# Requesting the cache pages of the compress stage during the input projection, and its first product as four 64x64 tiles

## The reference

```python
def compress(rows, pe, w1, w2):
    b, l, h, d = rows.shape
    nc = l // CMP_BLOCK                                   # CMP_BLOCK = 32
    blocks = rows.reshape(b, nc, CMP_BLOCK, h, d) + pe[None, None, :, None, :]
    flat = blocks.transpose(0, 1, 3, 2, 4).reshape(b, nc, h, CMP_BLOCK * d)
    return jax.nn.silu(flat @ w1) @ w2
```

## Time and profile before

| | before |
|---|---|
| time, median of 3 runs | 974.69 us (974.18 to 977.14) |
| the profiled execution's own time | 977.05 us |
| its span | 975.4 us |
| TensorE products (PE) | 918.1 us busy, 94% |
| TensorE weight loads (PEld, beside the products) | 692.2 us, 71% |
| VectorE (DVE) | 504.6 us, 52% |
| ScalarE (ACT) | 309.5 us, 32% |
| GpSimd (POOL) | 190.0 us, 19% |
| DMA | 91.11 MB, mean 93 GB/s |

### The profile page before, as it was taken

The page is one execution under the profiler, slowest core; times in us unless marked ns, Lnnn a source line. Parts: engine busy times, 40 slices in busy tenths (PEclk is TensorE's granted clock), DMA queues, the critical chain, the costliest instruction groups (busy, mean ns, idle before and its releaser), DMA issues. The chain is left out here.

```text
span 975.4 us, 15501 instructions
## 1 busy us (share of the span) xinstructions
PE 918.1 (94%) x5221; PEld 692.2 (71%) x5221; DVE 504.6 (52%) x1079; ACT 309.5 (32%) x691; POOL 190.0 (19%) x234
## 2 busy tenths in 40 slices
PE   7899999999999999999688898999999998989998
PEld 6676768887777787778588765566666655667784
DVE  4774254446165655340356366776666754564522
ACT  4222022213032424151200455655655543311100
POOL 1222222443002211110252001111011012443000
PEclk8999999999999999999899778999999999999999
DMA  7305811002530203113683500000000016888631
GB/s 264 133 19 106 226 29 59 1 2 86 211 103 1 87 10 122 44 50 106 149 193 99 151 1 23 22 23 23 1 23 10 13 31 208 234 227 293 212 97 48
DMA packets 90892, 91.11 MB, mean 93 GB/s; under 512 B 27629, under 2 KB 69533, under 8 KB 90453
## 3 DMA queue, kind: packets, MB, share of 16 engines
q1 hardware_dynamic: 70402, 71.60, 24.3%
q10 hardware_dynamic: 16700, 9.36, 3.6%
q0 software_dynamic: 3712, 9.17, 3.3%
HBM read 75.51 MB, written 23.49 MB: 101 GB/s over the span
## 5 line engine op out<-in xcount | busy, mean ns | idle before, releaser
L884 PE MATMUL ps<-w_high,x_high 128*128 128x512 f32 (+1 forms) x520 | 204.5, 393 | 2.3 <-DVE w_low L615 2.3
L886 PE MATMUL ps<-w_high,x_low 128*128 128x512 f32 (+1 forms) x520 | 199.5, 384 | 0.0
L885 PE MATMUL ps<-w_low,x_high 128*128 128x512 f32 (+1 forms) x520 | 199.1, 383 | 0.0
L884 PEld LDWEIGHTS ps<-w_high,x_high 128*128 128x128 f32 x520 | 97.8, 188 | 34.1 <-issue 12.9
L886 PEld LDWEIGHTS ps<-w_high,x_low 128*128 128x128 f32 x520 | 97.5, 187 | 21.0
L885 PEld LDWEIGHTS ps<-w_low,x_high 128*128 128x128 f32 x520 | 97.7, 188 | 18.9
L1721 PE MATMUL ps<-k_high,q_stack 128*128 128x512 f32 (+3 forms) x192 | 77.7, 408 | 11.9 <-DVE a_stats L1606 11.8
L399 POOL TENSOR_TENSOR stats<-stats,small 128x8 f32<-128x8 f32 (+3 forms) x35 | 41.7, 1190 | 206.4 <-DVE stats L667 158.5
L1721 PEld LDWEIGHTS ps<-k_high,q_stack 128*128 128x128 f32 x192 | 38.8, 202 | 53.3 <-DVE a_stats L1606 27.9
L1763 PE MATMUL ps<-weights_turned,v_nat 128*64 128x512 f32 x264 | 72.3, 629 | 0.0
L1722 PE MATMUL ps<-k_low,q_stack 128*128 128x512 f32 (+3 forms) x192 | 67.1, 356 | 0.0
(11 more groups left out here) (339 smaller groups left out, 1547.4 us busy)
## 6 DMA issues: line engine op xcount, KB each, us to landing
w_raw<-in_w_in SPq DMA_DIRECT2D x48, 256.0 KB, 4.5
tmp_skew<-tmp_table SPq DMA_DIRECT2D x8, 576.0 KB
bias_full<-tmp_skew SPq DMA_DIRECT2D x8, 512.0 KB, 4.8
w_out_raw<-in_w_out SPq DMA_DIRECT2D x16, 256.0 KB, 4.5
y_rows_in<-tmp_y SPq DMA_DIRECT2D x8, 512.0 KB, 4.8
x_rows<-in_x_prompt SPq DMA_DIRECT2D x8, 512.0 KB, 6.8
out_y_prompt<-out_rows SPq DMA_DIRECT2D x8, 512.0 KB, 6.7
x_tile<-in_x_prompt SPq DMA_DIRECT2D x6, 512.0 KB, 3.8
```

The source lines that it names most:

```text
L884: nc.tensor.matmul(out, s.xh[:, k, rows], s.wh[:, k, 0:w], start=(k == 0), stop=False)
L885: nc.tensor.matmul(out, s.xh[:, k, rows], s.wl[:, k, 0:w], start=False, stop=False)
L886: ins = nc.tensor.matmul(out, s.xl[:, k, rows], s.wh[:, k, 0:w], start=False, stop=(k == KT - 1))
```

## The change

1. The pages get room before the compress stage. Two units (`pages_early`) lie where `kct` and what follows it were; they are requested by SP in the q group. The other sixteen units, two of them prompt rows, lie in the columns of the input rows `x_high` and `x_low`: once zn has multiplied tile t, its columns are free, and two units go there. SP asks for four pages of each and POOL for the other four; ACT asks for none.
2. A page goes to 64 rows of SBUF, two consecutive rows of the page (two pieces of 512 bytes) to each, instead of 128 rows with one each. So two pages fill one 128-row tile, and its transposes give the even rows and the odd rows apart.
3. The prompt's rows are no longer transposed in the kv group; they are read back from the output `p_cmp_k` and `p_cmp_v` by SP in tiles 3 and 7 of zn, four requests each, as units like the others. So there are 18 units of two half units, 36 copies from PSUM, alternately on VectorE and ACT, over a ring of four banks.
4. The first product has no zeros: for each of 32 steps, four 64x64 products, two heads by even and odd block rows, into four quarters (two PSUM banks by upper and lower partitions). The weights stand in both halves of the partitions: SP loads them at the start of zn, VectorE copies them down in tiles 4 and 5. ACT copies one pair of quarters and VectorE adds the other to it, then silu follows.

The core of the diff:

```diff
+    s.w1 = Memory(nc, s.w_region).put("w1_doubled", [P, 2, CB, HD])
+    s.pages_early = Memory(nc, s.kct_region).put("pages_early", [P, EARLY, PAGES // 2, 2, KVW])
+    s.pages_in_x = [Memory(nc, s.x_region + 4 * KT * ROWS * part).put(f"pages_in_x{part}", [P, KT, ROWS]) for part in range(2)]
...
-                    if kind == "zn" and t < 2 * FIRST:
+                    if kind == "q" and t < 2 * EARLY:
                         if t == 0:
                             sp.wait_ge(table_in, 16)
-                            sp.wait_ge(w_low, KT * (g + 1))
-                        pool = io["cache_cmp_k"].rearrange("n t h d -> n t (h d)")
-                        for p in range(4 * (t % 2), 4 * (t % 2) + 4):
-                            at = PAGES * (t // 2) + p
-                            page = sp.value_load(s.pages[0:1, at:at + 1], min_val=0, max_val=N_PHYS - 1)
-                            sp.dma_start(s.raw_a[:, t // 2, p, :], pool[bass.ds(page, 1), :, :].rearrange("a t c -> (a t) c")).then_inc(s.c_first[t // 2], 16)
+                            sp.wait_ge(rows_in, 48)
+                            sp.wait_ge(r_out, TT)
+                        load_pages_paired(sp, s, io, t // 2, range(4 * (t % 2), 4 * (t % 2) + 4), s.early_in[t // 2])
+                    if kind == "zn" and t == 0:
+                        sp.wait_ge(w_low, KT * (g + 1))
+                        for kv, w1 in enumerate((io["cmp_w1_k"], io["cmp_w1_v"])):
+                            sp.dma_start(s.w1[0:HD, kv, :, :], dram(w1, 0, [HD, HD], [HD * HD, CB], [1, HD])).then_inc(s.w1_in, 16)
                     if kind == "zn":
                         sp.wait_ge(silu, NT + t + 1)
                         sp.dma_start(io["zn"][r0:r0 + n, :], s.st[0:n, slot, :]).then_inc(st_stored[slot], 16)
+                        if t < TT:
+                            for u in units_in(t):
+                                if is_prompt(u):
+                                    load_prompt_rows(sp, s, io, u, s.tile_in[t])
+                                else:
+                                    load_pages_paired(sp, s, io, u, SP_PAGES, s.tile_in[t])
...
+                    if kind == "zn" and t < TT:
+                        pool.wait_ge(table_in, 16)
+                        pool.wait_ge(projected, i + 1)
+                        for u in units_in(t):
+                            if not is_prompt(u):
+                                load_pages_paired(pool, s, io, u, POOL_PAGES, s.tile_in_sw[t])
...
+                    if KIND[g] == "zn" and t in (4, 5):
+                        dve.wait_ge(s.w1_in, 32)
+                        nc.vector.tensor_copy(s.w1[HD:P, t - 4, :, :], s.w1[0:HD, t - 4, :, :]).then_inc(s.w1_ready, 1)
...
                 if kind == "kv":
-                    for j in range(2):
-                        last = nc.tensor.transpose(s.ps[:, 3, P * j:P * j + n], st[:, KVW * j:KVW * j + KVW], one)
-                    last.then_inc(k_turned, 1)
...
-SLOTS, FIRST = 8, 4
-SP_PAGES, ACT_PAGES, POOL_PAGES = range(0, 3), range(3, 5), range(5, 8)
+EARLY, SEQS = 2, B + 1
+SP_PAGES, POOL_PAGES = range(0, 4), range(4, PAGES)
+is_prompt = lambda u: u % SEQS == B
+units_in = lambda t: (EARLY + 2 * t, EARLY + 2 * t + 1)
+
+
+def tile_of(s, u, q):
+
+    if u < EARLY:
+        return s.pages_early[:, u, q]
+    t, part = (u - EARLY) // 2, (u - EARLY) % 2
+    return s.pages_in_x[part][:, 2 * q:2 * q + 2, P * t:P * t + P]
+
+
+def load_pages_paired(engine, s, io, u, some, loaded):
+
+    pool = io[("cache_cmp_k", "cache_cmp_v")[u // SEQS]].rearrange("n t h d -> n t (h d)")
+    for p in some:
+        at = PAGES * (u % SEQS) + p
+        page = engine.value_load(s.pages[0:1, at:at + 1], min_val=0, max_val=N_PHYS - 1)
+        rows = slice(HD * (p % 2), HD * (p % 2) + HD)
+        engine.dma_start(tile_of(s, u, p // 2)[rows], pool[bass.ds(page, 1), :, :].rearrange("a (r two) c -> (a r) two c", two=2)).then_inc(loaded, 16)
+
+
+def load_prompt_rows(engine, s, io, u, loaded):
+
+    rows = io["prompt_out"][("cmp_k", "cmp_v")[u // SEQS]]
+    for q in range(PAGES // 2):
+        engine.dma_start(tile_of(s, u, q), dram(rows, 2 * KVW * P * q, [2 * KVW, P], [KVW, 2], [1, KVW])).then_inc(loaded, 16)
...
-        def load_pages(engine, u, some, loaded):
-
-            kv, b = u // B, u % B
-            if u >= SLOTS:
-                engine.wait_ge(turned, 2 * (u - SLOTS + 1))
-            for p in some:
-                page = engine.value_load(s.pages[0:1, PAGES * b + p:PAGES * b + p + 1], min_val=0, max_val=N_PHYS - 1)
-                engine.dma_start(raw(u)[:, p, :], pool_dram[kv][bass.ds(page, 1), :, :].rearrange("a t c -> (a t) c")).then_inc(loaded[u % SLOTS], 16)
...
-            b, half = i // 2 % B, i % 2
-            return view(kcs[:, 0, NBP * b + 16 * half:NBP * b + 16 * half + 1], [1, 16], [ALL, CB])
+            b = i // 2 % SEQS
+            return kcs[:, i % 2, :, NBP * b:NBP * b + NBP]
 
         def bank_of(i):
-            return view(s.ps[:, i % 3, 0:1], [CB, 16], [1, CB])
+            return view(s.ps[:, i % RING, 0:1], [1, CB // 2], [CB // 2, NBP])
...
+            def half_sums(kv):
+                act.wait_ge(first_out, 2 * kv + 2)
+                if kv == 1:
+                    act.wait_ge(silu_out, 1)
+                for h in range(HKV):
+                    frm = slice(HD * (1 - h), HD * (1 - h) + HD)
+                    nc.scalar.activation(both[HD * h:HD * h + HD, :], s.ps[frm, FIRST_BANK[kv][h], 0:ALL], ACT.Copy).then_inc(halved, 1)
...
+            def sums(kv):
+                dve.wait_ge(halved, 2 * (kv + 1))
+                for h in range(HKV):
+                    at = slice(HD * h, HD * h + HD)
+                    ins = nc.vector.tensor_tensor(both[at, :], s.ps[at, FIRST_BANK[kv][h], 0:ALL], both[at, :], ALU.add)
...
+            def turn(u):
+                landed(u)
+                for odd in range(2):
+                    i = 2 * u + odd
+                    if i >= RING and odd:
+                        pe.wait_ge(evacuated_a, kept_a(i - RING + 1))
+                    elif i >= RING:
+                        pe.wait_ge(evacuated, kept_v(i - RING + 1))
+                    for q in range(PAGES // 2):
+                        last = nc.tensor.transpose(s.ps[:, i % RING, P * q:P * q + P], tile_of(s, u, q)[:, odd, :], s.ident[:])
+                    last.then_inc(turned, 1)
...
-                for i in range(CB):
-                    if then and i % 4 == 0:
-                        turn_half(then + i // 4)
-                    last = nc.tensor.matmul(s.ps[:, 4 + kv, cols], w1[:, kv, i, :], kcs[:, i, cols], start=(i == 0), stop=(i == CB - 1))
+                    pe.wait_ge(position_kept, kv + 1)
+                pe.wait_ge(evacuated, kept_v(upto))
+                pe.wait_ge(evacuated_a, kept_a(upto))
+                for j in range(CB // 2):
+                    if then and j in (4, 10):
+                        for u in then.pop(0):
+                            turn(u)
+                    for odd in range(2):
+                        for h in range(HKV):
+                            at, to = slice(HD * h, HD * h + HD), slice(HD * odd, HD * odd + HD)
+                            last = nc.tensor.matmul(s.ps[to, FIRST_BANK[kv][h], cols], w1[at, kv, 2 * j + odd, :], kcs[at, odd, j, cols], start=(j == 0), stop=(j == CB // 2 - 1))
...
-            for i in range(B):
-                turn_half(i)
-            for kv in range(2):
-                for half in range(2):
-                    done = 2 * B * kv + B * (half + 1)
-                    first(kv, half, done if done < 4 * B else None)
-                    if kv == 1 and half == 0:
-                        second(0)
+            for u in range(4):
+                turn(u)
+            first(0, 0, [[4, 5], [6, 7, 8]])
+            first(0, 1, [[9, 10], [11, 12]])
+            first(1, 0, [[13, 14], [15, 16, 17]])
+            second(0)
+            first(1, 1, [])
```

More of the change, by code:

```diff
@@ L517, in post @@
                     br = 1 if kind == "wg" else 0
-                    act.wait_ge(k_turned, b + (1 if kind == "wg" else 2))
+                    act.wait_ge(k_turned, b + 1)
                     if t < TT:
@@ L1119, in compress @@
 def compress(nc, s, io):
-    m = Memory(nc, s.x_region)
[L1122 to L1126, removed]
+    ALL = NBS + NBP + 1
+    m = Memory(nc, s.w_region + 4 * 2 * CB * HD)
+    w1 = s.w1
+    kcs = m.put("kcs", [P, 2, CB // 2, ALL])
+    hid = m.put("hidden", [P, 2, NBS + NBP])
+    w2 = m.put("w2_blocks", [P, 2, P])
+    assert m.at <= SB_END
+    m = Memory(nc, s.rq_region + 4 * H * T + 4 * H * 2 * NBP)
+    both = m.put("both_parities", [P, ALL])
+    stat = m.put("c_stats", [P, 32])
+    assert m.at <= s.kct_region
+    m = Memory(nc, s.x_region)
     sq = m.put("c_squares", [P, 3, KVW])
@@ L1244, in _ @@
                 for j, (_, n) in enumerate(tiles):
+                    bank = OUT_BANK[j]
                     act.wait_ge(second_out, 3 * kv + j + 1)
```

(53 more changed lines are left out.)

127 lines of the change are left out of this document (45 added, 82 removed).

## The result

The changed kernel takes 999.62 us (996.38 to 1000.65, 4 runs), the kernel before 974.78 on the same chip: a ratio of 1.0248, interval 1.0221 to 1.0275. The profiled execution (996.38, span 994.7) is the shortest of the four, while that of before (977.05, span 975.4) was near the longest of its own; what the two traces differ by, 19.3 us, is therefore less than the 24.8 of the medians.

What follows compares the result with a forecast made beforehand. Projection was taken as bound by TensorE, compress by the arrival of pages, with SP all but full in zn. Barrier +46.1 us and compress -21.9 gave +24.2 on the median 974.69: 999 us, range 978 to 1020.

Steps and rivals of the forecast that it cites:

- SP's issue time: In zn, SP's page requests, stores and prompt reads last until 517.0, so barrier and compress come 46.1 us later.
- The price of the new request: In zn, a 64-row two-piece page request on SP was taken at 0.626 us, ends 0.338 and 0.697.
- a 64-row request costs no more: Rival, zn: a 64-row request costs SP no more than a 128-row one; +8.1 us, 983; chance 0.18.
- Compress: Compress stage: no idle time on pages, products four at once; 47.3 us against 69.2, 21.9 shorter.
- the wait for the last copy from PSUM: In compress, TensorE waits at four places for the last evacuation, 0.17 + 1.09, 4.7 us in all.
- The tail: End of compress: ACT copies and VectorE adds 0.45 each, hand-overs 0.4, silu 0.55, second product 1.0, copies 1.25 us.
- Transfers did not set the pace: Rival, zn: transfers, not requests, set the pace, until 487; shift 16.2, sum -5.7 us, 969; chance 0.05.
- Products run four at a time, not two: Rival, compress: only two products at once, 0.136 each; stage 64.5 us, sum +41.4, 1016; chance 0.10.
- TensorE was at half speed: Rival, compress: TensorE stays at half clock throughout; stage about 75 us, +52, 1027; chance 0.05.
- kv and q groups, silu, POOL: kv 1.8 us earlier, q nothing; in zn tile 7's silu about 488 and POOL's end 491, both before SP.

Runs made afterwards that it cites:

- 128 rows: Changed kernel, but a page goes to 128 rows of SBUF instead of 64 rows with two pieces: 986.99 us, ratio to before 1.0141.
- the three cures together: Changed kernel with 128-row pages, pages of zn tiles 0 to 5 shared by SP, ACT, POOL, tiles 6 and 7 behind the barrier: 952.52 us, ratio 0.9795.
- two quarters: Changed kernel, but both products of a head write that head's own quarter, using two quarters of TensorE, not four: 1017.23 us, one run.

## Why the prediction was right, point by point

**SP's issue time.** Forecast: through at 517.0; measured 517.1, and compress 46.5 later for 46.1. The runs above show the mechanism, not only the number: the same requests shared out, cheaper ones, or behind the barrier gave back 27, 10 and 22 us by the ratios, where 33, 10 and 25 to 30 were expected. The agreement to a tenth of a microsecond is luck: the eight tiles took 87.0 us for 85.3, and the first store went out at 429.6, where the sum began at 431.3, so two misses of 1.7 cancel. Inside the 87.0, too, terms missed both ways. The page was taken at 1.382 and cost 1.30 to 1.36 (10.08 - 0.54 over 7, or 9.62), because the request took 0.538 and not 0.626. Against that, the first tile took 13.7 us for 11.5 (its store alone 2.96, behind the two weight loads; why was not tested), a prompt read 0.61 for 0.51, and a store 0.59, for which 0.47 stood.

**The price of the new request.** 0.538 lies between the ends 0.338 and 0.697, nearer to the dear one; the rival "a 64-row request costs no more" falls. When the cheap request was put in (128 rows), SP was through 34.6 us later than before (505.5 for 470.88), not the 30.0 of that rival: the first tile took 11.6 us for 9.2, and the other full tiles 9.3 to 9.9, while the two with prompt reads took the 6.9 of the sum.

**Compress.** Forecast 47.3 us, measured 44.35; 21.9 shorter against 24.9. The term that was mis-sized most is the wait for the last copy from PSUM: four places and 4.7 us were taken (four times 0.17 + 1.09 would be 5.0), and TensorE waited at two, 0.79 and 1.68, 2.5 us in all. A copy took 0.69 (VectorE) and 0.61 (ACT), where 1.09 stood. The products took 17.3 us for 18.6, at 0.064 for 128 columns and 0.072 for 161 (4.61 over 64), where 0.068 and 0.0775 stood. The transposes took 18.6 for 18.0. The tail was right: 560.06 to 564.99, 4.9, against 5.0.

**The rivals.** Transfers did not set the pace (128 rows, and the three cures together). Products run four at a time, not two; the price of two was forecast at 0.136 and is 0.118, and 1017 with two quarters, one run, agrees with the 1016 of that rival. TensorE was at half speed for the first transposes only, and its mean clock was 0.96 over the stage.

**kv and q groups, silu, POOL.** As forecast they cost nothing. TensorE's last products ahead of the barrier came 3.6 us earlier (466.07 for 469.71), where 1.8 were forecast; in the traces of the other eight kernels it is 1.4 to 3.8. TensorE loses it again, since SP is through later. The silu of tile 7 came at 488.5 (488 in the text), POOL's last request at 492.5 (491), both ahead of SP.

**What was not foreseen** is how much single executions differ: the changed kernel and the one that reads page numbers in one go, with SP through within one us of each other, were profiled with spans of 994.7 and 1002.3. Of the 7.6 us some 3 lie in compress and its end and 4 in the stages behind, where the granted clock was 0.79 for 0.81 in the first 73.6 us. What decides this is open.

## What to carry to other kernels

A request that is moved ahead of a barrier is not hidden by the busy engine beside it once the engine that issues it has no time left: for each engine, count requests times issue time up to the barrier, the reading of an index into a register included. When an engine of many has to issue everything, share it among the engines whose lists have room, and let what is needed late be asked for behind the barrier. The shape of a transfer (rows and pieces) changed its issue time on SP here, though bytes and count of pieces were equal.

## What the runs showed of the hardware

- Asking for 64 KB took SP 0.338 us into 128 rows, 0.468 into 64 rows of one piece and 0.538 into 64 rows of two pieces (medians). The 128x512 store behind the pages took 0.43 beside the first form and 0.59 beside the last. On POOL the same shapes made little difference: 0.544 for 128 rows, 0.585 for 64 rows of two pieces.
- Reading one number into a register and bounding it took 0.77 us, and four in a row, each with its bound, 3.06.
- A copy of 512 columns from PSUM took 0.69 us on VectorE whether it read at every 16th element and wrote runs of 32, or (in the kernel with 128 rows) read at every 32nd and wrote runs of 16. The copies of before, which wrote single elements 289 apart, took 1.08. The scattered write was the price, not the scattered read.
- Behind POOL's last request a barrier opened after 5.9 us (one trace). Behind SP's last store it was 3.4 to 3.5 us (changed kernel, 128 rows, numbers in one go), of which 1.6 in the changed kernel's trace are a wait for that store to land.
